# Gated attention by levels: exponents as products of stored gates with 0/1 interval matrices, and 64x64 score blocks

## The reference, cut to what matters

```
def step(s, inp):
    qc, kc, vc, gc = inp
    cum = jnp.cumsum(gc.astype(jnp.float32), axis=1)
    inter = jnp.einsum("blhk,bhkv->blhv", qc * jnp.exp(cum), s)
    diff = cum[:, :, None] - cum[:, None, :]
    decay = jnp.exp(jnp.where(mask[None, :, :, None, None], diff, -jnp.inf))
    att = jnp.einsum("bihk,bjhk,bijhk->bhij", qc, kc, decay)
    intra = jnp.einsum("bhij,bjhv->bihv", att, vc)
```

## Time and profile before

| | us |
|---|---|
| median of 3 runs | 3476.84 (3476.39 to 3479.95) |
| the profiled execution | 3473.43 |
| its span | 3471.6 |
| TensorE matmul busy | 3310.9 (95% of the span) |
| VectorE busy | 1896.5 (55%) |
| ScalarE busy | 1403.5 (40%) |
| GpSimd busy | 257.4 (7%) |
| mean granted TensorE clock | 0.981 |

### The profile page before, as it was taken

One profiled execution on the slowest core, in us unless ns is written; L12 is line 12 of the kernel. 1 busy time (PEld: TensorE's weight loads), 2 busy tenths in 40 slices (PEclk: granted clock), 3 DMA queues, 4 the chain that ended last, 5 costly groups with the idle time before them and its releaser, 6 DMA issues.

```text
span 3471.6 us, 45331 instructions
## 1 busy us (share of the span) xinstructions
PE 3310.9 (95%) x17843; PEld 2635.8 (76%) x17843; DVE 1896.5 (55%) x2490; ACT 1403.5 (40%) x2239; POOL 257.4 (7%) x265
## 2 busy tenths in 40 slices
PE   6799887899999999999999999999999999999999
PEld 6576655777778878789965559999999655687887
DVE  6777587856534443536565564454545645644433
ACT  4532454444332332324435553343334355533322
POOL 1000033310000000000021000010000300000000
PEclk9999988999999999999999999999999999999999
DMA  6444201014333234323210112342342001123333
GB/s 238 155 152 159 69 22 58 13 61 154 93 118 121 85 98 161 100 87 119 90 43 7 36 40 80 98 162 84 122 148 72 34 7 43 38 90 124 113 91 115
DMA packets 95893, 321.40 MB, mean 93 GB/s; under 512 B 11248, under 2 KB 12672, under 8 KB 95168
## 3 DMA queue, kind: packets, MB, share of 16 engines
q1 hardware_dynamic: 75392, 246.52, 22.3%
q0 software_dynamic: 18752, 67.71, 5.6%
q10 hardware_dynamic: 1536, 4.26, 0.3%
HBM read 295.26 MB, written 23.20 MB: 92 GB/s over the span
## 4 chain that ended last, share of the span: by engine, by line
PE 82%; DVE 11%; ACT 4%; DMA 1%; issue 1%; POOL 0%; DVEq 0%; ACTq 0%; POOLq 0%
PE psum L146 80%; DVE mixer L175 4%; DVE mixer L185 2%; PE psum L149 2%; DVE wlo L175 1%; DVE arena L175 1%; DVE junk L189 1%; DVE mixer L202 1%; ACT whi L163 1%; DVE region L175 0%; DMA mixer<-in_wm 0%; DVE stage L175 0%; ACT mixer L154 0%; ACT arena L154 0%; DMA stage<-in_wi 0%
## 5 line engine op out<-in xcount | busy, mean ns | idle before, releaser
L146 PE MATMUL psum<-region,whi 128*128 128x260 f32 (+2 forms) x7616 | 1833.8, 334 | 6.5 <-DVE region L185 3.2
L146 PEld LDWEIGHTS psum<-region,whi 128*128 128x128 f32 (+1 forms) x7616 | 1278.8, 186 | 173.3 <-DVE region L175 9.6
L146 PE MATMUL psum<-region,wlo 128*128 128x260 f32 (+2 forms) x3808 | 1265.8, 332 | 0.0
L175 DVE TENSOR_TENSOR wlo<-stage,whi 128x1024 fp32r<-128x1024 f32 (+2 forms) x454 | 512.7, 1129 | 639.1 <-ACT whi L163 601.8
L146 PEld LDWEIGHTS psum<-region,wlo 128*128 128x128 f32 (+1 forms) x3808 | 711.2, 187 | 78.5
L163 ACT CAST whi<-stage 128x1024 fp32r<-128x1024 f32 (+2 forms) x454 | 442.2, 974 | 247.3 <-PE psum L146 160.0
L154 ACT ACTIVATE arena<-psum 128x512 f32<-128x512 f32 (+2 forms) x412 | 193.5, 470 | 722.0 <-PE psum L146 717.4
L146 PE MATMUL psum<-arena 128*128 128x512 f32 (+11 forms) x1072 | 382.4, 479 | 0.0
L163 ACT COPY arena<-psum 128x260 f32<-128x260 f32 (+9 forms) x345 | 154.4, 447 | 370.1 <-PE psum L146 353.7
L175 DVE TENSOR_TENSOR arena<-arena 128x512 f32<-128x512 f32 (+8 forms) x341 | 212.2, 622 | 139.9 <-ACT arena L154 129.0
L175 DVE TENSOR_TENSOR arena<-arena,psum 128x512 f32<-128x512 f32 (+1 forms) x220 | 126.2, 574 | 283.7 <-PE psum L146 275.7
(11 more groups left out here) (155 smaller groups left out, 2868.3 us busy)
## 6 DMA issues: line engine op xcount, KB each, us to landing
stage<-in_w SPq DMA_DIRECT2D x144, 512.0 KB, 3.5
stage<-in_wi SPq DMA_DIRECT2D x55, 512.0 KB, 4.4
stage<-in_wo SPq DMA_DIRECT2D x48, 512.0 KB, 3.6
stage<-in_wg SPq DMA_DIRECT2D x44, 512.0 KB, 3.4
stage<-in_wu SPq DMA_DIRECT2D x44, 512.0 KB, 3.4
stage<-in_wm SPq DMA_DIRECT2D x42, 512.0 KB, 3.5
stage<-in_wd SPq DMA_DIRECT2D x32, 512.0 KB, 3.4
arena<-xr_scratch POOLq DMA_DIRECT2D x5, 2080.0 KB, 9.7
```

Source lines behind the costliest of these rows:

```text
L146: return Issued(self, self.e and self.e.matmul(out, w, x, start=start, stop=stop, skip_group_check=True))
L175: return Issued(self, e and e.tensor_tensor(out, a, b, op))
```

## The change

Four things change.

1. The exponents. The sum of gates between a row and a boundary is a sum over an interval of rows. For each distance and direction a 0/1 matrix over the 128 rows of a tile says which rows belong to it. GpSimd makes these 2 x 7 matrices early in the SSD stage (`pool_intervals`, 35 small operations) and stores them (`IS`, 128 x 2 x 7 x 128); the gates of tiles 2 to 9 are stored from `gtk` by SP (`GS`). Both are loaded again for each half of the rows: `gq` (the gates of four tiles), `sums_of` (the matrices). TensorE multiplies them into banks 2 to 5, and ScalarE takes the exponential from there, with scale 1/16, straight into `expo`. The work comes in 64 units (half and pair of heads, part p of 4, tile jj): part 0 holds distance 64 (128 columns for each direction), parts 1 to 3 two distances each (256 columns). Two units go into each round, four ahead. VectorE's subtractions and the second exponential are gone.
2. The scores. Only the 64x64 blocks that a level needs are made, 16 matmuls of 64x64 in place of 8 of 64x128, into one pair of banks (0, 1), and copied into a compact buffer `attc` (512 elements a partition); GpSimd places it in `att` once in 8 levels. ScalarE copies distance 64 alone; 32 is masked like the others.
3. The dummy products are gone.
4. Times of the rounds, and waits: the queries' exponentials come in rounds 0, 1, 2, 5 and their products in 9, 17, 25, 33; outputs start in rounds 19, 23, 27, 31; the first low half of `wo` comes in the last round, behind GpSimd's last placement, since `attc` lies over the weight halves.

```
+    gq, sums_of = (at(19600, 4, 512), cut(hold, 0, (4, 512))), (at(21648, 2, 7, 128), cut(hold, 2048, (2, 7, 128)))
+    made = at(23776, 2, 7, 128)
+    attc = (cut(hold, 7552, (2, 4, 64)), cut(hold, 6144, (2, 4, 64)))
...
+    def pool_intervals(e):
...
+        for l, Bs in enumerate((1, 2, 4, 8, 16, 32, 64)):
...
+                e.tensor_tensor(S, S, C[f"m{Bs // 2}"], ALU.add).then_inc(*G.up())
+            for d, sides in enumerate((("gt", "le"), ("ge", "lt"))):
+                for two, c in enumerate(sides):
...
+        e.dma_start(IS, made).then_inc(*ist.up("out", by=16))
...
 def dve_gates / dve_ssd
+            if t >= 7:
+                e.wait_ge(*gst[0]["end"])
...
+                if j == 0:
+                    e.wait_ge(*ist["out"])
...
 def sp_ssd
+        for t in range(2, 10):
+            e.wait_ge(*sgla.dve["gtk", t])
+            e.dma_start(GS[:, t - 2, :], gtk[t % 5]).then_inc(*gst[t > 4].up(by=16))
...
+        e.wait_ge(*sssd.pe["in", 7])
+        e.wait_ge(*ist["out"])
+        e.dma_start(sums_of[0], IS).then_inc(*ivd[0].up("in", by=16))
+        e.wait_ge(*gst[0]["end"])
+        e.dma_start(gq[0], GS[:, 0:4, :]).then_inc(*gld[0].up("in", by=16))
...
-    OUT_AT = {19: 0, 22: 1, 25: 2, 28: 3}
-    Q_AT = {3: 0, 27: 1}
+    OUT_AT = {19: 0, 23: 1, 27: 2, 31: 3}
+    Q_AT = {0: (0, 0), 1: (0, 1), 2: (1, 0), 5: (1, 1)}
+    PARTS_OF_LEVELS = [(g, p, jj) for g in range(4) for p in range(4) for jj in range(4)]
+    def units_at(r):
+        return [u for u in (2 * r + 4, 2 * r + 5) if u < len(PARTS_OF_LEVELS)]
...
+    def pe_part(e, u):
...
+        b, free = bank.take(("part", u), A, "ex", u, among=(2, 3, 4, 5))
...
+        for d in range(2):
+            c = sums_of[q4][:, d, max(2 * p - 1, 0):2 * p + 1, :]
+            out = psum[:, b, 0:512 if p else 256].rearrange("p (x d c) -> p x d c", d=2, c=64)[:, :, d, :]
+            ins = e.matmul(out, gq[q4][:, jj, (2 * d + f) * 128:(2 * d + f + 1) * 128], c, True, True)
...
+    def act_part(e, u):
...
+        if jj == 0 and u >= 8:
+            for Bs in {0: (8, 4), 1: (2, 1), 2: (64,), 3: (32, 16)}[p]:
+                n = 8 * ((u - 8) // 16) + [x[1] for x in LEVEL[0:8]].index(Bs)
+                e.wait_ge(*G["qs", n])
+                if Bs > 1:
+                    e.wait_ge(*D["ks", n])
...
 def pe_gla
-        for s, n, r in with_outputs(pe_round, e):
-                pe_fill(e, (6, 7), 5)
+        for r in range(NL + 4):
+            for u in parts[0:1]:
+                pe_part(e, u)
+            n = r - 2
-                b, free = bank.take(("lv", n), A if whole(n) else D, "lv", n, n=2, align=2, among=(0, 1, 2, 3))
+                b, free = bank.take(("lv", n), A if Bs == 64 else D, "lv", n, n=2, align=2, among=(0, 1))
...
+                            ins = e.matmul(psum[kh * 64:kh * 64 + 64, b + hf, jj * 64:jj * 64 + 64],
+                                           ks[r_, k0:k0 + 64], qs[r_, q0:q0 + 64], True, True)
+            for u in parts[1:2]:
+                pe_part(e, u)
+            pe_round(e, r)
...
 def act_gla
+            for u in parts[0:1]:
+                act_part(e, u)
+            n = r - 3
+            if 0 <= n < NL and LEVEL[n][1] == 64:
+                for kh in range(2):
+                    e.copy(att_block(n, kh, 1 - kh), compact(n)[kh * 64:kh * 64 + 64]).then_inc(*A.up())
...
 def dve_gla
-                        e.tensor_tensor(planes_of(sl_, d, Bs), c, ref[...], ALU.subtract)
+            n = r - 1      # the keys' product, waits for A["ex", last_part(n)] and T["lv", before(n)]
+            n = r - 3      # the copy: 128 x (2, 4, 64) into attc
...
 def dve_round
-        if r == NL + 1:
+        if r == NL + 3:
+            e.wait_ge(*sgla.pool["placed", 3])
             dve_weights(e, W, W.last["wo", 0, 0])
...
 def pool_gla
+            n = r - 4
+            if 0 <= n < NL and n % 8 == 7:
+                e.wait_ge(*D["lv", n])
+                for kh in range(2):
+                    e.tensor_copy(att_block(n, kh, kh), attc[n // 8 % 2][kh * 64:kh * 64 + 64])
```

More of the change, by code:

```diff
@@ L507, in mixer @@
     K.yd = [K.sig(f"y_in{i}") for i in range(2)]
+    gst, gld, ivd = ([K.sig(f"{n}{i}") for i in range(2)] for n in ("gates_out", "gates_in", "intervals_in"))
+    ist = K.sig("intervals_out")
     def xp(m):
@@ L1542, in level_in, with compact, att_block @@
         return s, lo, f, Bs, q4, ql, kl
[L1545 to L1550, removed]
+    def compact(n):
+        b = bank.of["lv", n]
+        return psum[:, b:b + 2, 0:256].rearrange("p a (j c) -> p a j c", c=64)
+    def att_block(n, ks, qs):
         f, Bs, q4 = LEVEL[n]
[L1552 to L1558, removed]
+        return att[ks * 64:ks * 64 + 64, f, :, q4 * 4:q4 * 4 + 4, qs * 64:qs * 64 + 64]
@@ new lines, in last_part, with q_planes, k_planes, part_sums @@
+    def last_part(n):
+        return 16 * (n // 8) + 4 * PART_OF[LEVEL[n][1]][0] + 3
+    def q_planes(n, Bs):
+        return expo_of(n)[:, 256:768].rearrange("p (two g b) -> p g two b", two=2, b=Bs)
+    def k_planes(n, Bs):
+        return expo_of(n).rearrange("p (pl n) -> p pl n", n=256)[:, 0:4:3, :].rearrange("p two (g b) -> p g two b", b=Bs)
+    def part_sums(u):
+        p = PARTS_OF_LEVELS[u][1]
+        w = psum[:, bank.of["part", u], :]
+        if p == 0:
+            return w[:, 0:256].rearrange("p (q c) -> p q c", c=64)
+        return w.rearrange("p (l q c) -> p l q c", l=2, c=64)
@@ L1626, in pe_turn @@
         T, A, D = sgla.pe, sgla.act, sgla.dve
-        b, free = bank.take(("turn", j), D, "out", j, among=(6, 7) if j < 4 else (2, 3))
+        b, free = bank.take(("turn", j), D, "out", j, among=(6,) if j < 4 else (2, 3))
         for x in free:
@@ L1708, in act_round @@
         if r in Q_AT:
[L1709 to L1713, removed]
+            q4, d = Q_AT[r]
+            e.wait_ge(*sssd.dve["end"])
+            if q4 and d:
+                for c, last in ((ogd[0], 6), (ogd[1], 7)):
+                    e.wait_ge(*c[last])
+            e.activation(qc[q4][:, d], cum[:, d * 2:d * 2 + 2, 256 + q4 * 512:768 + q4 * 512], ACT.Exp).then_inc(
+                *A.up("q", q4, d))
         for what, j in outputs_at(r):
@@ L1727, in act_gla @@
         T, A, D, G = sgla.pe, sgla.act, sgla.dve, sgla.pool
[L1728 to L1737, removed]
+        e.wait_ge(*sssd.pe["end"])
+        for r in range(-2, NL + 4):
+            parts = units_at(r)
+            for u in parts[0:1]:
+                act_part(e, u)
+            n = r - 3
+            if 0 <= n < NL and LEVEL[n][1] == 64:
                 e.wait_ge(*T["lv", n])
-                e.wait_ge(*D["lv", n // 8 * 8])
-                for dst, src in quadrants(n):
-                    e.copy(dst, src).then_inc(*A.up())
+                for kh in range(2):
+                    e.copy(att_block(n, kh, 1 - kh), compact(n)[kh * 64:kh * 64 + 64]).then_inc(*A.up())
                 A.mark("lv", n)
+            for u in parts[1:2]:
+                act_part(e, u)
+            act_round(e, r)
         e.wait_ge(*D["lv", NL - 1])
@@ L1780, in dve_gla @@
+        for r in range(NL + 4):
+            n = r - 1
+            if 0 <= n < NL and LEVEL[n][1] > 1:
+                sl_, lo, f, Bs, q4, ql, kl = level_in(n)
+                e.wait_ge(*A["ex", last_part(n)])
                 if before(n) is not None:
                     e.wait_ge(*T["lv", before(n)])
-                e.tensor_tensor(by_halves(qe[:, sl_, 1, :], Bs), k_planes(sl_, Bs), by_halves(kl, Bs),
+                e.tensor_tensor(by_halves(qe[:, sl_, 1, :], Bs), k_planes(n, Bs), by_halves(kl, Bs),
```

151 lines of the change are left out of this document (86 added, 65 removed).

## The result

The changed kernel takes 3487.7 us (median of 6 runs, 3482.7 to 3492.0), the kernel before 3478.1 in the same setting: ratio 1.0027, interval 1.0014 to 1.0040. It is slower by 9 us (by the ratio; 9.6 by the medians) where I forecast 8 us less. A second profiled execution of it (e0_after) took 3488.4.

What follows compares the result with a forecast made beforehand. VectorE bounded the levels stage; afterwards TensorE and the one-pair score loop would. Terms 6.2 + 97 + 13 + 3 + 5.0 + 2 + 1 = 127 for 137.5 us, hand-overs giving 3 back: 3469 us, range 3455 to 3494.

Steps and rivals of the forecast that it cites:

- (a): Score matmuls on TensorE: quadrants do not pair, scores take 2.0 us, +28 us, 3497; chance 15%.
- (b): Levels: VectorE's key product and GpSimd's query product lock after the same matmuls, +15 us, 3484; chance 15%.
- The head: Stage start to first scores: TensorE does units 0 to 8, 6.2 us, with the loads hidden.
- The stall of level 64: Once in eight levels ScalarE's copy waits behind a unit needing GpSimd's query product: 5.1 us for 3.05.
- The slow start of the output projection: Behind the tail's idle time TensorE runs at a lower clock, so the output projection loses 2 us.
- The tail from the last scores: Last scores to output projection: scores 1.1, copy 0.8, GpSimd's placements 0.9, low half of weights 1.25; 5.0 us.
- A round: TensorE's cost for two big units and one level's scores: 0.88 x 2 + 1.29 = 3.05 us.
- low bound: Scores of a level, limited by issue alone: 32 small matmuls 26 ns apart, 0.83 us.
- the first 17 gaps: Time from the first score group to level 17; the forecast's split gives 53.8 us.
- the outputs' term: Second part of the stage: four products and turns add 13 us, VectorE's output work 3 us.
- The last 14 gaps: Score groups from level 17 to level 31, outputs included; the forecast's split gives 59.2 us.
- a loop of four operations: One bank pair: scores 1.1, wake-up 0.05, key product 0.80, copy 0.73, hand-overs 0.14; 2.8 us a turn.

Runs made afterwards that it cites:

- e0_after: The changed kernel once more with no edit, for a second profile (also written e0); 3488.4 us, ratio 1.0026.
- after: The changed kernel itself, unedited, against the kernel before; 3487.7 us, ratio 1.0027.
- e7: Changed kernel without the product, squares, scaling and turn of the first four attention outputs; 3457.1 us, ratio 0.9944.
- e3: Changed kernel with five filling matmuls ahead of each score group from round 19 on; 3488.0 us, ratio 1.0029.
- c3: e1 with the first 38 exponent units through banks 4 to 7, and the third and fourth turns in banks 4 and 5; 3470.8 us, ratio 0.9979.
- c4: c3 with the splits of the state-space rows in rounds 18, 22, 26, 30 instead of 20, 23, 26, 29; 3465.5 us, ratio 0.9969.
- c5: c4 with twelve filling matmuls ahead of products 1 to 3, before their wait for banks 6 and 7; 3460.2 us, ratio 0.9950.
- c2: e1 and e3 together: two pairs of banks plus the five filling matmuls; 3478.3 us, ratio 1.0000.
- e1: Changed kernel with scores through two bank pairs (0,1) and (2,3) in turn, exponent units through 4 and 5 alone; 3473.1 us, ratio 0.9984.
- e4: Kernel before with its score groups on the one pair of banks 0 and 1 instead of two pairs; 3503.8 us, ratio 1.0076.
- e5: Changed kernel with ScalarE copying the level-64 scores ahead of both exponent units instead of between them; 3478.6 us, ratio 1.0009.

## Why the prediction was wrong

**What held.** 3487.7 us lies inside my range of 3455 to 3494, and that is luck: the upper part of the range stood for rivals (a) and (b), and neither happened. The subtractions went, VectorE is busy 52.4 us (55 forecast), and TensorE heads the chain (67%). The head took 6.1 us (6.2): the loads were in time. The stall of level 64 took 4.7 in its second place (5.1), link by link as forecast: the scores end at 635.8, GpSimd's query product, then the unit, then the copy, then the scores at 639.83:

```profile
635.95 1.78 POOL L175 TENSOR_TENSOR mixer<-mixer 128x512 f32<-128x512 f32 x1 [0.18 <-PE psum L146]
```

```profile
637.95 0.60 ACT L154 ACTIVATE mixer<-psum 128x512 f32<-128x512 f32 x1 [0.42 <-PE psum L146]
638.58 1.19 ACT L163 COPY mixer<-psum 64x512 f32<-64x512 f32 x2
```

(The unit's wait is put down to TensorE, which was long done; GpSimd ended at 637.73.) In its first place it took 5.0 for another reason, ScalarE's query exponentials, and each was followed by a gap of 4.2, the lower clock, which I had not. The slow start of the output projection is there: eight records 0.43 us apart for 0.23, 1.5 us (2). The tail from the last scores took 5.9 (5.0): VectorE's scaling of the last output (1.5) came ahead of the copy, the placements took 1.28, not 1.8. The additions to the stage ahead are hidden (1, bounds 0 and 3). A start of the stage after 600 us, one of my signs of being wrong, says nothing: it starts at 602.9 in after, at 599.3 in e0, the same kernel, and the stage takes 150.6 in both.

**What TensorE costs was set too high.** Four quadrants overlap: 32 records in 0.69 us, 0.62 to the start of the next unit, where I took 1.25 with the changes of shape. A change costs some 0.1 us on either side (0.31 and 0.32 us between two starts for 0.215). A round is 8 x 0.215 for the units and 0.83 for scores and changes, 2.55 us, not 3.05. Rival (a) fell; 0.69 is below even my low bound of 0.83. The 26 ns a matmul behind that bound does not hold over four quadrants: the 32 records start 19 ns apart in the mean. The Trainium skill, "TensorEngine Tiling (Array Packing)", 64×64 Mode, lists four tiles, and its Key Properties say that tiles operate independently; the run agrees, and I had taken two. With that the first 17 gaps took 49.5 for 53.8. Rival (b) fell too: key products took 0.77 in the mean, query products 1.53 for 1.34, a lock now and then, on GpSimd's side.

**The step that failed** is the outputs' term: "Outputs: four products of 4.3 and four turns of 0.7 [...] 13 us", with "VectorE's output work shifts four key products behind GpSimd: 3 us". I added TensorE's own time and one engine's. The last 14 gaps took 89.1 for 59.2, and this 30 us is more than the whole miss of 23 in the stage. e7 measures the term: 34.2 for 16. Without the outputs the 14 gaps still take 54.9 us for 43.2, 12 more; the splits and the lower clock, which had no term at all, lie there, and no run splits the 12 between them. I had seen the single pair and made it a loop of four operations; I did not ask what else stands in the two lists between a score group and the copy that frees its banks. Each entry there (unit, squares, cast, split) is a link of the ring. The runs that change this alone move the time: a second pair takes 17.5 us off the stage (22.3 in the gaps, with 4.8 lost in head and tail), an earlier copy 10, and taking the second pair from the old kernel costs it 25.

The ring over banks 0 and 1 isn't the whole of the 30 us. With the second pair the 14 gaps still take 75.2 for 59.2; turns in other banks bring them to 73.8 (c3), later splits to 71.9 (c4), fills ahead of the products to 64.3 (c5). The last 5 stay open. So does what outputs cost in the kernel before, which no run measures; there the turns had banks 6 and 7 and the products 4 and 5, while the changed kernel has the products in 6 and 7 and the turns in 6. c3, which moves two of the four turns out of bank 6, took 1.4 us off the 14 gaps.

The same rule, to rotate independent matmul groups through different PSUM banks so that evacuation overlaps the next group, is in the Trainium skill, "Perfetto Trace Analysis", Matmuls; the runs agree: 17.5 us gained and 25 lost.

**The clock** had a term for the tail alone. It is the second part of what is left: in after, behind the waits of 1.98 and 2.19 us ahead of the second and third product, TensorE runs at the lower level (1.2 GHz) for most of a product. Fills ahead of every score group from round 19 on raised it and gave nothing (e3) or cost time (c2); filling exactly the wait ahead of two products gives 5 to 8 us (c5), which shows that there the wait set the clock. How much of after's 30 us is clock and how much is wait I can't split: no run had the one without the other there.

**Whole kernel against stage.** Stage differences against before (+13.1, -4.4, +24.8, +2.6, -22.6, -11.6, -19.4 for after, e1, e4, e5, e7, c4, c5) and those by the ratios (+9, -6, +26, +3, -19.5, -11, -17) agree within 4 us, which is what an interval leaves. Nothing outside this stage needs explaining.

## What to carry to other kernels

Where one buffer is shared by a producer and in-order consumers, count every instruction that stands between its filling and its release in the consumers' lists, also those that have nothing to do with it; their sum, not the busiest engine, can be the period of the loop. Here operations of half the length did not pay for the pair of banks that was given up with them: look at the banks first, at the operations second. Filling matmuls paid here only inside a wait that stood ahead of a long group; look for a group that takes 1.6 times its usual time right behind a wait.

## What the runs showed of the hardware

Score matmuls of 64x64 start in fours, one in each quadrant: in after at 658.45 the records of a four start 6 to 8 ns apart, and from the second on a four starts 58 ns behind the one before (32 records in 0.69 us at 2.4 GHz, 1.13 at 1.2 GHz). Behind waits of 2.0 to 3.3 us a product's 24 records took 5.6 to 7.6 us for 4.2 (every second and third product of after and of the runs made from it, but for e7, which has none, and c5), and behind one of 2.07 two units took twice their time; behind one of 1.71 (e5) they did not. The length of the wait alone doesn't decide it: in e7 score groups and units ran at full speed behind waits of 2.1, 2.8 and 2.8 us (at 665.28, 674.90 and 685.37). With the wait ahead of a product filled, the product ran at full speed.
